# Three lo parts and the last sum of squares move from VectorE to GpSimd at the entry of an FFN

## The reference

```python
def rmsnorm(x, g):
    xf = x.astype(jnp.float32)
    y = xf * lax.rsqrt(jnp.mean(xf * xf, axis=-1, keepdims=True) + EPS)
    return (y * g.astype(jnp.float32)).astype(x.dtype)

def sq_relu_mlp(h, w1, w2):
    return jnp.square(jax.nn.relu(h @ w1)) @ w2
...
        x = x + cross_attend(rmsnorm(x, P['norm_x_g'][l]), mem_k[l], mem_v[l], P['w_xq'][l], P['w_xo'][l])
        x = x + sq_relu_mlp(rmsnorm(x, P['norm_ffn_g'][l]), P['w_ff1'][l], P['w_ff2'][l])
```

## Time and profile before

| | µs |
|---|---|
| median of 3 runs | 2259.76 (2259.72 to 2261.11) |
| profiled execution | 2257.59 |
| its span | 2255.9 |
| TensorE busy | 2181.3 (97%) |
| VectorE busy | 1237.0 (55%) |
| GpSimd busy | 823.7 (37%) |
| ScalarE busy | 595.9 (26%) |

### The profile page before, as it was taken

The page is one execution under the profiler, slowest core; times in us unless marked ns, Lnnn a source line. Parts: engine busy times, 40 slices in busy tenths (PEclk is TensorE's granted clock), DMA queues, the critical chain, the costliest instruction groups (busy, mean ns, idle before and its releaser), DMA issues.

```text
span 2255.9 us, 34688 instructions
## 1 busy us (share of the span) xinstructions
PE 2181.3 (97%) x14272; PEld 2119.9 (94%) x14272; DVE 1237.0 (55%) x1417; ACT 595.9 (26%) x947; POOL 823.7 (37%) x599
## 2 busy tenths in 40 slices
PE   6999999999999999999999999998999999999997
PEld 5998899999999999999999986798999999899997
DVE  5558899653121222213455263269988886864763
ACT  5331222122101010111111172014333334333334
POOL 6114100004444434444444302145544444544541
PEclk9999999999999999999999999999999999999999
DMA  7522332122212112111311214321443448744322
GB/s 211 150 75 84 130 113 99 58 87 98 67 57 66 58 57 67 47 47 46 117 47 47 92 30 168 113 91 58 161 154 131 144 147 271 246 152 157 120 70 80
DMA packets 220344, 237.59 MB, mean 105 GB/s; under 512 B 8120, under 2 KB 181176, under 8 KB 218151
## 3 DMA queue, kind: packets, MB, share of 16 engines
q1 hardware_dynamic: 201814, 203.17, 27.9%
q10 hardware_dynamic: 18145, 32.57, 4.2%
q0 software_dynamic: 256, 0.01, 0.0%
HBM read 177.53 MB, written 58.67 MB: 105 GB/s over the span
## 4 chain that ended last, share of the span: by engine, by line
PE 88%; DVE 6%; DMA 2%; ACT 1%; issue 1%; POOL 0%; ACTq 0%; SPq 0%; DVEq 0%; POOLq 0%
PE PS L1057 53%; PE PS L1496 13%; PE PS L1543 13%; PE PS L1444 1%; PE PS L1406 1%; DVE opnd L2668 1%; DVE slots_d L2232 1%; PE PS L1377 1%; PE PS L1126 1%; PE PS L1088 1%; DMA xring<-in_x_prompt 1%; PE PS L1419 1%; PE PS L1362 1%; DVE w_lo L2255 1%; DMA hid_scratch<-stage 0%
## 5 line engine op out<-in xcount | busy, mean ns | idle before, releaser
L894 POOL TENSOR_TENSOR w_hi<-w_raw,ones 128x512 fp32r<-128x512 f32 x150 | 175.7, 1171 | 802.8 <-PE PS L1057 757.6
L1543 PE MATMUL PS<-opnd,slot 128*128 128x272 f32 x2688 | 342.5, 289 | 4.9 <-DVE opnd L2668 3.6
L1496 PE MATMUL PS<-opnd,slot 128*128 128x272 f32 x2688 | 341.2, 289 | 5.5 <-DVE opnd L2668 2.0
L1496 PEld LDWEIGHTS PS<-opnd,slot 128*128 128x128 f32 x2688 | 339.5, 189 | 6.9 <-issue 4.5
L1543 PEld LDWEIGHTS PS<-opnd,slot 128*128 128x128 f32 x2688 | 340.3, 189 | 5.7 <-DVE opnd L2668 4.1
L1057 PE MATMUL PS<-h_hi,w_hi 128*128 128x364 f32 x1512 | 337.1, 331 | 6.1 <-DVE w_lo L2255 5.8
L1057 PE MATMUL PS<-h_hi,w_lo 128*128 128x364 f32 x1512 | 334.0, 329 | 0.0
L1057 PE MATMUL PS<-h_lo,w_hi 128*128 128x364 f32 x1512 | 333.9, 329 | 0.0
L959 POOL TENSOR_TENSOR slot<-raw_A,slot 128x512 fp32r<-128x512 f32 x160 | 239.5, 1503 | 242.0 <-ACT slot L1556 241.6
L2503 DVE TENSOR_TENSOR tmp<-PS,tmp 128x728 f32<-128x728 f32 x64 | 43.4, 720 | 431.3 <-PE PS L1057 431.3
L1057 PEld LDWEIGHTS PS<-h_hi,w_hi 128*128 128x128 f32 x1512 | 260.5, 188 | 12.0 <-issue 10.1
(11 more groups left out here) (323 smaller groups left out, 3107.8 us busy)
## 6 DMA issues: line engine op xcount, KB each, us to landing
w_raw<-in_w_in SPq DMA_DIRECT2D x64, 512.0 KB, 4.0
hid_scratch<-stage SPq DMA_DIRECT2D x16, 1904.0 KB, 6.6
opnd<-hid_scratch SPq DMA_DIRECT2D x56, 544.0 KB, 6.4
raw_A<-in_w_ff SPq DMA_DIRECT2D x64, 256.0 KB, 3.1
raw_A<-in_w_ff SPq DMA_DIRECT2D x32, 512.0 KB, 4.6
branch_scratch<-oring ACTq DMA_DIRECT2D x16, 544.0 KB, 2.8
xring<-in_x_prompt SPq DMA_DIRECT2D x16, 512.0 KB, 6.0
w_raw<-in_w_branch SPq DMA_DIRECT2D x16, 512.0 KB, 3.5
```

The source lines that it names most:

```text
L894: nc.gpsimd.tensor_tensor(w_hi[:, z % 2, cols], w_raw[:, z % 2, cols], ones[:, 0:1].broadcast_to([P, 512]), ALU.mult).then_inc(w_hi_done, 1)
L1496: mm = mmul(product_of(u, p)[:, c, :], w, x[:, HC * c:HC * c + HC], start=(j == 0 and e == 0), stop=(j == PAIRS - 1 and e == 2))
L1543: mm = mmul(product2_of(t)[:, c, :], w, x[:, part, HC * c:HC * c + HC], start=(j == 0 and e == 0), stop=(j == 2 * PAIRS - 1 and e == 2))
```

## The change

Three of the sixteen late lo parts, those of product 3's pairs 0 to 2, leave VectorE's list for GpSimd's, with a semaphore of their own. They keep their hi copies in the old order on ScalarE. The add of the last tile's squares leaves VectorE for GpSimd too. Both stand in GpSimd's stream behind the lo part of slot 5 and ahead of that of slot 3. VectorE's groups of late lo parts are cut anew (positions 3 to 5, 6 to 8 and the rest of a list of 13), so that its PSUM reads stand where they stood.

```diff
+LATE_POOL = [(3, 0), (3, 1), (3, 2)]
+LATE_DVE = [x for x in LATE if x not in LATE_POOL]
...
         weight_lo(0, 5)
+        for p, j in LATE_POOL:
+            pool.wait_ge(late_hi, LATE.index((p, j)) + 1)
+            add(opnd[p][:, j, 1, :], late_source(p, j), opnd[p][:, j, 0, :].bitcast(F32),
+                ALU.subtract).then_inc(late_lo_pool, 1)
+        pool.wait_ge(res_sq, 2 * KT)
+        pool.wait_ge(sumsq, 10 + KT - 1)
+        add(tmp[0][:, :], tmp[0][:, :], tmp[2][:, :], ALU.add).then_inc(sumsq, 1)
         weight_lo(0, 3)
...
             else:
-                pe.wait_ge(late_lo, LATE.index((p, j)) + 1)
+                if (p, j) in LATE_POOL:
+                    pe.wait_ge(late_lo_pool, LATE_POOL.index((p, j)) + 1)
+                else:
+                    pe.wait_ge(late_lo, LATE_DVE.index((p, j)) + 1)
...
             if u < 2:
-                act.wait_ge(late_lo, len(LATE))
+                act.wait_ge(late_lo, len(LATE_DVE))
+                act.wait_ge(late_lo_pool, len(LATE_POOL))
...
         def late_operand_lo(i):
-            p, j = LATE[i]
-            dve.wait_ge(late_hi, i + 1)
+            p, j = LATE_DVE[i]
+            dve.wait_ge(late_hi, LATE.index((p, j)) + 1)
...
-            if m == KT - 1:
-                squares_summed()
...
-        for i in range(3, N_LATE_EARLY + 3):
+        for i in range(3, 6):
             late_operand_lo(i)
         p6_added(0)
-        for i in range(N_LATE_EARLY + 3, N_LATE_EARLY + 6):
+        for i in range(6, 9):
             late_operand_lo(i)
         hidden_11_added(0)
-        for i in range(N_LATE_EARLY + 6, len(LATE)):
+        for i in range(9, len(LATE_DVE)):
             late_operand_lo(i)
```

More of the change, by code:

```diff
@@ L542, in _build @@
     x_t, late_hi, late_lo = S("x_t"), S("late_hi"), S("late_lo")
+    late_lo_pool = S("late_lo_pool")
     wino = S("wino_product")
@@ L2743, in hidden_11_added @@
             if u == 0:
-                dve.wait_ge(late_lo, LATE.index((3, 3)) + 1)
+                dve.wait_ge(late_lo, LATE_DVE.index((3, 3)) + 1)
             if u >= 1:
```

## The result

| | before | after |
|---|---|---|
| median, µs | 2259.31 (22 runs, 2256.26 to 2261.11) | 2262.20 (22 runs, 2259.93 to 2264.37) |
| ratio after/before, 95% interval | | 1.0014 [1.0009, 1.0020] |
| the same, measured a second time | 2259.96 (33 runs) | 2262.23 (11 runs), 1.0014 [1.0005, 1.0023] |

The change costs 3.2 µs (2.0 to 4.5). The forecast was +3.9. A difference counts as over 0.2% from 4.5 µs on, so the case is one of "within 0.2%", though the sign is certain: both intervals lie above 1.

A forecast was written before the change was run, and what follows sets the result against it. TensorE was taken as the bound (88% of the chain), so VectorE and GpSimd work counts only where it stands still. Terms 5.7 + 0.3 - 0.8 - 1.35 = +3.85, say +3.9 µs: median 2263.7, range 2258.0 to 2266.0.

The forecast's parts named there:

- Turns are taken, and a longer GpSimd operation blocks longer: VectorE ahead of product 6's last lo part: three waits of 1.15 and one of 2.3, TensorE's stall +5.7 µs.
- The operation of 4.25: Start of the kernel: a VectorE operation taking 4.25 µs beside two GpSimd ones, cited for waits growing with GpSimd's operation.
- The sum: 5.7 + 0.3 - 0.8 - 1.35 = +3.85 µs, say +3.9; median 2263.7, +0.17%.
- The operations removed don't shorten the stall: VectorE's removed 3.28 µs stand after product 6's last lo part, so TensorE's 1.83 stall there doesn't shrink by them.
- Half clock, +0.3: The 30 matmuls behind product 6's stall: 0.3 µs more than before for the longer stall, bounds -1.55 and +1.3.
- Given back, -0.8 and -1.35: Products 7 and 5 find lo parts ready, -0.8 µs; the wait ahead of the sample sum goes, -1.35.
- The copy of product 1: ScalarE's copy waits for the add and ends four µs later, at 1550.3; later copies and slots stay covered.
- After the sample sum, 0: Both later TensorE gaps of 1.11 µs stay: 0, bounds -2.2 and +2.2; the shift is carried to the end.
- A: Rival: GpSimd's four operations don't hinder VectorE; sample sum moves by -2.15 µs, median 2257.6; chance 0.12.
- C: Rival: a fixed wait for each VectorE operation, 4.5 µs in place of 5.7; +2.7, median 2262.4; chance 0.12.
- B: Rival: VectorE locked out in full and the clock stays low; +5.65 µs, median 2265.4; chance 0.26.

The follow-up runs named there:

- add only: From the kernel before: only the add of the last squares moves to GpSimd, the three lo parts stay on VectorE; ratio 1.0007 [0.9997, 1.0016].
- lo parts only: From the kernel before: only product 3's three lo parts move to GpSimd, the add stays on VectorE; ratio 1.0000 [0.9991, 1.0009].
- held back: The changed kernel with GpSimd's four operations starting only once product 6's last lo part is made; ratio to before 1.0016 [1.0007, 1.0025].
- three parts later: From the kernel before: VectorE's three late lo parts move from behind tile 6 to behind tile 7, nothing goes to GpSimd; ratio 1.0003 [0.9994, 1.0012].
- both of these: From before: product 4's lo parts on GpSimd, VectorE's three late ones behind tile 7, product 2's ahead of product 3's; ratio 0.9987 [0.9978, 0.9996].
- product 4's parts: From before: product 4's four lo parts go to GpSimd behind unit 1's first weight sum, the add stays on VectorE; ratio 0.9987 [0.9978, 0.9996].

## Why the prediction was right

*Turns are taken, and a longer GpSimd operation blocks longer.* Predicted 1.15 three times, then 2.3. Measured 1.05, 1.14 and 1.02 over the 0.72, then 3.52 - 1.36 = 2.16 in the kernel after and 2.3 with the add only. The last lo part was due 5.7 later and came 5.35 later. Undoing each half gives its victims back, holding all four back gives back the 1.83, and operations that read nothing leave the two-input ones alone, so this is shown, not argued.

The support for the longer block was weaker than the prediction took it. The operation of 4.25 is a TENSOR_SCALAR with one tensor from SBUF, and L2701 is one too, yet the prediction let the collisions begin behind it, with L2709. That L2701 was spared was luck of the order: its counterpart started 0.09 ahead of GpSimd's first lo part. With the lo parts only it started 0.20 behind it and took 1.74. Already the trace of before had such a case one tile earlier:

```profile
1529.21 1.70 DVE L2701 TENSOR_SCALAR x_res<-x_res,vec_b 128x1088 f32<-128x1088 f32 x1
```

```profile
1527.98 2.35 POOL L959 TENSOR_TENSOR slot_f<-s_tmp,raw_A 128x512 f32<-128x512 f32 x1
```

The sum hardly hung on it: in the kernel with the lo parts only the gain was the first of three victims in place of the last block sum, and the stall grew by the 3.1 of three waits all the same.

The Trainium skill, "SBUF — State Buffer", section "Who interferes with whom", has the VectorE instruction blocked until GpSimd's finishes. The trace agrees: in the kernel after the add ended at 1553.17 and the two lo parts beside it, which take 1.36 when nothing is beside them, at 1554.40; with the add only a lo part waited 2.3 µs for an add of 2.72.

*The operations removed don't shorten the stall.* Right: with the collisions gone and the same list removed, the stall was 1.83 (held back).

*Half clock, +0.3.* The term that was mis-sized most, and a guess between two bounds. The 30 matmuls took 0.76 more, inside the bounds of -1.55 and +1.3. The low clock lasted 10.24 µs, three times as long as before, though half of it fell into the stall. The 0.46 too little here and the 0.35 too much at the stall nearly cancel, which is luck.

*Given back, -0.8 and -1.35, together -2.15.* Measured -1.95. Both parts came as said: products 7 and 5 run without a wait and no wait stands before the sample sum. The whole of products 7 and 5 with their tail now takes 6.43, and the three other kernels whose stall is longer than before's show 6.43 or 6.42 too.

*The copy of product 1.* Its start was due at 1549.7 on before's clock, and it started at 1553.27 - 3.82 = 1549.45. Slots 3 and 4 were due at 1552.6 and began at 1552.30. Nothing waited for either. VectorE's L2561 was due to end at 1563.4 and ended at 1562.4, of which 0.5 is that the collisions with the slots and the weight sum cost 2.7 and not 3.2, and 0.3 that the last lo part of product 6 came sooner. VectorE then waited 2.47 for the sample sum, so that this error stayed free. In the kernel held back the wait for the slots and the weight sum sat on the path, cost 2.2 and made most of the miss.

*After the sample sum, 0.* The gaps are 1.12 and 1.10, and the shift of 4.05 at unit 1 is still there at the second matrix.

*The sum.* 5.35 + 0.76 - 1.95 = 4.16 for a predicted 3.85. The medians moved by 2.9 and the ratio says 3.2 (2.0 to 4.5), so both the predicted 3.9 and the 4.1 read at the entry lie within the interval. The median was forecast at 2263.7 and is 2262.20; 0.45 of that is that before has a median of 2259.31 in 22 runs, and not the 2259.76 of the first three. Whether anything lies between 4.1 and 3.2 isn't settled; the varying stretch at the second matrix is as large as that.

*The rivals.* A needed L2709 to stay at 0.72: it took 1.77. What A described does happen where GpSimd reads nothing (-1.33 from tile 7's gain, L2714's loss of 0.61 included). C needed the lo part behind the add at 1.8; the two take 3.52, and with 0.67 for the other it took 2.9. B, a full lock-out, needed 6.5 of blocking, L2701 at several µs and a low clock on all 30 matmuls: the stall grew by 5.36, VectorE got its turn between any two of GpSimd's operations, and the 30 matmuls took 0.76 more and not 1.3.

## What to carry to other kernels

An idle GpSimd is not free capacity. An operation of GpSimd that reads SBUF delayed the VectorE operation of two SBUF inputs beside it by most of its own length: here 5.4 µs of blocking for 3.28 µs of work taken over. Look at what VectorE does at the moment at which the moved work will run, not at where the work was: ahead of the last operand that TensorE stands for it cost 4.2 µs, beside a PSUM read and a wait the same kind of work won 1.5. And when a change has several parts, slack is spent once: two halves that cost 1.2 and 1.6 cost 4.2 together. Before two traces are compared to a tenth of a µs, see whether the engines met in the same way ahead of the change: here that alone was 0.35.

## What the runs showed of the hardware

- Two engines with full lists alternate one for one: 1.77, 1.86 and 1.74 for VectorE's three operations beside GpSimd's three. GpSimd pays too, but less: 1.83 instead of 1.35 for a lo part, where VectorE pays 1.75 to 1.86 instead of 0.72.
- A write-only operation of GpSimd is not harmless to all. Beside memsets of 0.70 and 1.00 the two-input ops kept 0.72 and 1.36, but the TENSOR_SCALAR, one input from SBUF, took 1.40 instead of 0.79; a memset had started 0.21 ahead of it. For this operation it matters who starts first. Where GpSimd's started later, by 0.09 to 0.67 µs, it took 0.79 (the kernel after, three parts later, both of these). Where GpSimd's had started 0.20 ahead it took 1.74, and for tiles 0 to 6, where GpSimd's had started 1.1 to 1.24 ahead and had 1.1 to go, it took 1.7 in every trace.
- The length of the half clock doesn't follow the stall alone. A stall of 1.83 behind a gap of 1.24 gave 3.41 µs of it, 4.11 and 4.95 gave 6.83, and 7.19 gave 10.24. A stall of 1.83 behind a gap of 0.88 gave 3.41 (held back), and one of 1.84 behind a gap of 0.90 none at all (product 4's parts), so that the gap ahead doesn't explain it either. What does stays open.
